# Another order for the table of portions in the second block of a fused two-block transformer kernel

## What is computed

```
h = rmsnorm(x, attn_norm)
c_q, c_kv, k_r, q_d, k_d, v_d = split(h @ w_in)      # 384, 256, 32, 512, 512, 512 columns
q  = rmsnorm(c_q)  @ w_uq        # 8 latent heads of 96
kv = rmsnorm(c_kv) @ w_ukv       # k (64) and v (64) of each; 32 rotated columns of k come from k_r
o_a = softmax(rope(norm(q)) rope(norm(k))^T) v        # 8 latent heads
o_b = dilated attention over q_d, k_d, v_d with a relative bias   # 8 dilated heads
x = x + concat(o_a, o_b) @ w_out
x = x + conv_ffn(rmsnorm(x))
```

## Time and profile before

| | |
|---|---|
| runs | 1645.78, 1648.69, 1649.99 us; median 1648.69 |
| profiled execution | 1644.55 us, span 1642.8 us |
| TensorE matmul / weight load | 1589.0 us (97%) / 1463.2 us (89%) |
| VectorE / ScalarE / GpSimd | 1129.8 us (69%) / 919.0 us (56%) / 127.2 us (8%) |
| first dense matmul of the table to T0 | layer 0: 993.7 to 1116.7 us; layer 1: 1320.3 to 1443.3 us |

### The profile page before, as it was taken

How to read it: one execution, slowest core, us unless ns; L and a number is a source line. 1 busy time by engine, 2 the same in 40 slices (tenths; PEclk the granted TensorE clock), 3 DMA queues, 4 the chain that set the end, 5 groups by cost and what they waited for, 6 DMA issues and landing times. The chain is left out here.

```text
span 1642.8 us, 31046 instructions
## 1 busy us (share of the span) xinstructions
PE 1589.0 (97%) x12874; PEld 1463.2 (89%) x12874; DVE 1129.8 (69%) x1763; ACT 919.0 (56%) x1459; POOL 127.2 (8%) x106
## 2 busy tenths in 40 slices
PE   6999999999999999999999999999999999999999
PEld 3987478999999999966899999878999998799999
DVE  2799677645566655897765556778887567788873
ACT  3444756545365444647554446767666467676662
POOL 0230000112001100300011000000101000001110
PEclk9999999999999999999999999999999999999999
DMA  9443666656546555435566653323555533245553
GB/s 395 160 152 131 258 236 227 235 216 240 192 167 221 205 188 201 155 125 207 195 228 237 220 184 119 118 78 130 207 191 202 204 112 116 77 137 200 207 193 118
DMA packets 46172, 303.36 MB, mean 185 GB/s; under 512 B 5072, under 2 KB 7376, under 8 KB 12752
## 3 DMA queue, kind: packets, MB, share of 16 engines
q1 hardware_dynamic: 45312, 299.78, 50.7%
q0 software_dynamic: 288, 0.92, 0.1%
q10 hardware_dynamic: 432, 0.68, 0.1%
HBM read 298.22 MB, written 3.15 MB: 183 GB/s over the span
## 5 line engine op out<-in xcount | busy, mean ns | idle before, releaser
L2002 DVE TENSOR_TENSOR wl<-raw,wh 128x1040 fp32r<-128x1040 f32 (+1 forms) x472 | 576.4, 1260 | 295.8 <-ACT wh L1759 229.9
L1759 ACT ACTIVATE wh<-raw 128x1040 fp32r<-128x1040 f32 (+1 forms) x472 | 466.5, 1031 | 195.5 <-PE bank L1552 109.3
L1547 PE MATMUL bank<-hx_hi,wh 128*128 128x256 f32 x1856 | 519.6, 280 | 6.0 <-ACT hx_hi L1759 3.8
L1552 PE MATMUL bank<-hx_lo,wh 128*128 128x256 f32 x1856 | 516.2, 278 | 0.0
L1550 PE MATMUL bank<-hx_hi,wl 128*128 128x256 f32 x1856 | 514.7, 277 | 0.3 <-DVE wl L2002 0.2
L1547 PEld LDWEIGHTS bank<-hx_hi,wh 128*128 128x128 f32 x1856 | 349.0, 188 | 10.8 <-issue 9.8
L1550 PEld LDWEIGHTS bank<-hx_hi,wl 128*128 128x128 f32 x1856 | 349.1, 188 | 2.8 <-issue 1.7
L1552 PEld LDWEIGHTS bank<-hx_lo,wh 128*128 128x128 f32 x1856 | 348.8, 188 | 1.0 <-DVE hx_lo L1995 0.4
L1550 PE MATMUL bank<-hid_hi,wl 128*128 128x256 f32 x912 | 252.2, 277 | 1.4 <-DVE wl L2002 1.4
L1547 PE MATMUL bank<-hid_hi,wh 128*128 128x256 f32 x912 | 252.5, 277 | 0.3 <-ACT wh L1759 0.2
L1552 PE MATMUL bank<-hid_lo,wh 128*128 128x256 f32 x912 | 251.9, 276 | 0.0
(11 more groups left out here) (218 smaller groups left out, 1891.5 us busy)
## 6 DMA issues: line engine op xcount, KB each, us to landing
raw<-in_wts SPq DMA_DIRECT2D x208, 1032.0 KB, 4.9
raw<-in_wts SPq DMA_DIRECT2D x50, 1024.0 KB, 6.6
raw<-in_wts SPq DMA_DIRECT2D x20, 776.0 KB, 4.3
raw<-in_wts SPq DMA_DIRECT2D x4, 584.0 KB, 4.4
tscr<-tmp SPq DMA_DIRECT2D x4, 512.0 KB, 7.4
bias<-tscr SPq DMA_DIRECT2D x4, 512.0 KB, 6.0
raw<-in_wts SPq DMA_DIRECT2D x2, 648.0 KB, 4.0
xTc<-in_ctxT SPq DMA_DIRECT2D x1, 1024.0 KB, 10.6
```

Source lines behind the costliest of these rows:

```text
L1547: pe.matmul(out, block(f, M.wh, w0 + k, ncols, c, m), x_hi, start=first and k == 0 and o == 0, stop=False, skip_group_check=True)
L1552: ins = pe.matmul(out, block(f, M.wh, w0 + k, ncols, c, m), x_lo, start=False, stop=last and k == nk - 1, skip_group_check=True)
L1759: return act.activation(out, in_, func, bias=bias, scale=scale)
L2002: tt(M.wl[k][:, cols], M.raw[r][:, cols], M.wh[k][:, cols].bitcast(F32), ALU.subtract).then_inc(*on.inc(lo))
```

## The change

Only the table `BETWEEN` changes; no step is added or removed.

```diff
-BETWEEN = ("h r D0 h L0 L2 N r r D2 D4 r D3", "", "D1 r r Q0", "K0", "", "s K1 h s V Q1", "r r", "s r D5 h h", "h r",
-           "Q3 Q2 h", "", "s K2 r r r K3 h", "s", "r O0 h O1 s", "", "O2", "", "h O3 h", "h", "h s T0 T1 T2 T3 h")
+BETWEEN = ("h r D0 h D2 r L0 r", "L2 N D4", "D3 r", "D1 r r Q0", "K0 s r", "r Q1", "K1 r h", "r D5 r h", "V h",
+           "Q2 K2 h", "r r Q3 h", "K3 r r O0 h", "O1 s", "h", "O2 h", "h", "O3 h", "h", "h", "h s T0 T1 T2 T3 h")
```

## The result

The kernel after takes 1707.05 us (median of 4 runs, 1705.25 to 1709.36), before 1648.3 beside it: ratio 1.0358, 95% interval 1.034 to 1.0377. The prediction said slower and had the direction, but its size was half of what came: +30.3 us forecast (1679 on 1648.69), +58.7 measured, and 1707 lies outside the range of 1663 to 1694.

The account below looks back on a forecast made before the run. Matmuls bound the kernel, so only TensorE's waits can change. Five steps sum to 17.2 us a layer, taken as 15.0, plus 0.7 for the clock; twice 15.7 is 31.4, forecast 1679 us, range 1663 to 1694.

Parts of the forecast that it names:

- Scores 0: Row 0: scores come right behind D2's rest, so TensorE waits for q and k; +2.2 us a layer.
- Latent rest: Rows 1 to 3: moved behind D3, it makes TensorE wait, mostly 7.4 us for D1's square; net +6.4 us a layer.
- Rows 4 to 10: Spread Q and K work makes turned 3 wait about 3.5 us, less 2.2 for double rests; net +1.9 a layer.
- O0's split: Row 11: O0's piece is split only directly ahead of its matmuls; 4.0 us wait less 2.8, net +1.2 a layer.
- The tail: Rows 12 to 18: dense pieces in even rows leave turns 13, 15, 17 waiting; net +5.5 us a layer.
- second rival: Whole table: queues clear during row 3's wait, so later waits shrink; about +8 us a layer, 1665 us; chance 0.17.
- clock term: Behind the 7.4 us wait for D1's square the clock falls once a layer, half hidden; +0.7 us a layer.
- first rival: The clock falls at every wait over 3 us (D1's square, turned 3, O0, turned 15); 1690 us; chance 0.12.
- waits overlap more: Turned 3 and the tail wait less since queues clear in row 3; about +8 us a layer, 1665; chance 0.17.
- the latent rest finds its cover: Row 3: D1's square is not held up, so removed waits decide; -2 to -4 us a layer, 1642; chance 0.03.
- it cancels: Whole table: the queues catch up everywhere and the kernel stays within its old waits, 1649 us; chance 0.04.
- A: Experiments' theory, D0 to T0: clock falls cost time of their own beside the waits, some 8 to 10 us a layer.

Follow-up runs that it names:

- e5: The new table with D2's rest ahead of L0 instead of behind it (row 0): 1698.42 us, ratio 1.0315 to the kernel before.
- e6: The new table with 18 constant matmuls a layer added in the long TensorE waits, each fill meant to be shorter than its wait: 1699.22 us, ratio 1.031.
- e12: The new table with 7 constant matmuls added in the wait at D1's small matmul alone: 1703.10 us, ratio 1.034.
- e1: The new table with the latent rest back directly behind N, ahead of D4 and D3 (rows 1 and 2): 1690.22 us, ratio 1.0266.
- e8: The new table with rows 11 to 18 in the old order, D2's rest ahead of L0 and the latent rest directly behind N: 1659.67 us, ratio 1.007.
- e7: The new table with rows 11 to 18 in the order of the kernel before: 1684.36 us, ratio 1.0215.
- e2: The new table with O0 one row later (row 12), so its piece can be split ahead: 1708.21 us, ratio 1.0375.
- e9: The kernel before with double rests and O0 spread as in the new table (rows 9 to 13): 1648.54 us, ratio 1.0006.
- e4: The new table with 38 constant matmuls a layer added in seven long TensorE waits: 1707.40 us, ratio 1.037.
- e11: The kernel before with O2 moved to row 14 and O3 to row 16: 1654.34 us, ratio 1.0045.

## Why the prediction missed the size

**By steps, layer 0.**

1. *Scores 0*: right. 2.2 forecast, 2.28 measured; e5 shows it can be had back by cover alone.
2. *Latent rest*: right. D1's square 7.4 against 6.95, PSUM 1.2 against 1.42. The 1.1 at scores 2 isn't there: with the clock at 0.50 Q0 took 4.6 us (2.5 in the kernel before), and the product was ready. At full clock it is 0.2 (0.18 in e6, 0.16 in e12), so the term was too large in any case. e1 takes the step back and wins what it says (6.4 forecast, 7.6 and 6.5).
3. *Rows 4 to 10*: turned 3 waited 2.29, forecast 3.5, the 0.6 behind it did not come. The 2.2 that was subtracted for the double rests was never a wait, so the net of +1.9 came near the 2.3 measured by luck. e8 has 4.0 us of waits more than the kernel before: 2.3 at turned 3, the rest in rows 1 to 3 (1.1) and the tail (0.6).
4. *O0's split*: 4.0 forecast, 2.40 + 1.43 measured: right. What was set against it, 2.8 in row 11, was 1.2. The reason, a split that starts too late, is borne out by e7, where the piece is whole before O0 and 0.59 is left; e2, which has only half of it split ahead, gains nothing.
5. *The tail*: 2.2, 2.6, 3.4 forecast, 1.95, 2.24, 1.69 measured, and 0.73 for values 7 as said. The last was half of its forecast: VectorE had nothing queued by then (1.55 us idle ahead of the split half at 1142.14), which is what the second rival had right.
6. *T0 to T3*: forecast untouched, 1.1 us longer in layer 0, by the fall that the last waits left behind.

**The two steps that failed.** Against 15.7 us a layer stand 28.6 measured (mean of both): 18.5 of waits, 8.8 of clock and 1.4 of rest. The waits were 3.5 short (2.2 of it because I took 15.0 for the 17.2 that the list gave), the clock 8.1, and the rest, whose cause stays open, was not forecast at all. The new waits came to 29 by my list and to 23.3 by the trace. The first failing step is the *subtraction*: 11.8 us of waits were to go with the old table (3.4 in rows 1 to 3, 2.2 for the double rests, 2.8 in row 11, 3.4 in the tail), but there were only 5.0 in it (1.0, 0, 1.2 and 2.8). The prediction added up a layer from start-to-start times, got 106 us and called the missing 14 to 17 "waits and hand-overs". The list of waits, which gives 5.0 in four lines, was not weighed against that sum; with the busy 118.0 it makes up the 123.0, so the busy column hid no wait. Part of the error lay in the 512-column f32 matmuls of the rests: their price was read as the distance to the next record (1025.38 to 1025.83), while the pair takes 0.86 us. The stretch has 12 of them, which makes 5 of the 12 us between 106 and 118.0. Another part may be the dense pieces: the stretch holds 480 such matmuls, ten times 48 with O0 to O3, and the sum names eight; as it isn't written out, this stays open. The 3.26 us of the latent rest are work (14 records, two of them D0's rest, and no gap in the list of waits), not 1.8 of work and 1.4 of wait, and e9 moves the double rests for nothing. Overcounts on both sides happened to cancel, which is luck: 17.2 net forecast (15.0 taken), 18.3 measured.

The second, and the one that made the miss, is the *clock term*: 0.7 us a layer forecast, 9.6 and 8.0 measured. I put one fall behind the longest wait alone and took half of it as hidden. In layer 0 five came, at waits of 1.7 to 7 us, each of 3 to 10 us, and TensorE was busy for some 19 us of the layer at 1.2 GHz; layer 1 had four. That is my first rival's mechanism, with a chance of 0.12, but it too counted only waits over 3 us, at 1.5 us each; the 1690 that it gave was 17 us short. Its argument against (before holds 1.00 through waits of 1 us) said nothing of waits of 2. The Trainium skill (TensorE: Matmul & The Clock Gate, Part 1) says that the throttled state is the default and activity releases it; the falls at turned 13 and 15 agree with it, more than I let it count, while turned 3, with 2.29 us, had none.

**The rivals.** That waits overlap more (1665) was right for the tail and turned 3 and worth 6 us a layer of new waits, offset by the 7 us of waits that were falsely subtracted. That the latent rest finds its cover (1642) is out: the chain took 9.8 us. That it cancels is out; the `h` of rows 7 to 10 are indeed no-ops in both (the `s` of row 7 before is not: it makes the split at 1066.25).

**What was only bounded.** The loss at half clock is an upper bound of what it costs. Taken back, 6.9 us of it gave 4.8 (e6), and waits and fills together grew by 1.6: the two half splits of ScalarE at 1052.89 took 1.99 us within the fall, as long as at full clock (2.00 at 1037.23 in the kernel before), so a TensorE that comes sooner waits longer for the other engines. That falls cost time beside the waits, A's mechanism, is shown by e4, e6, e7 and the first layer of e11; the size that A gave them, 8 to 10 us a layer, is not. From e6, about 70% of the 8.8 us mean loss, 6 us a layer, is what the clock really cost, and waits and rest make the other 22 to 23 (an estimate).

## What to carry to other kernels

Before subtracting a wait, find it in the list of waits of the kernel before: a sum of instruction prices that falls short of the stretch can be work that was priced too low, as part of it was here, and not a wait. For a change of order, count the TensorE work between handing something to ScalarE or VectorE and asking for it back, and put the queue of both engines into that time; that gave each new wait to about 1 us here, the last one in the tail to 1.7. Then price the clock: where new waits of about 2 us came here, a half-clock stretch of 3 to 7 us followed most of them, 10 us with the longest. It cost about a quarter of the waits on top of them (6 of 23 us a layer, an estimate), and in the tail up to nearly as much as the waits (5.1 against 5.7 in layer 0 of e7, 3.4 against 6.2 in layer 1). And take a move of cover alone before several together: K1 beside K0 gave 0.9 us a layer, the set that held it lost 4.6.

## What the runs showed of the hardware that was not expected

- The granted clock fell to 0.50 behind waits as short as 1.69 + 0.73 us (turn 15 and values 7) and 1.95 us (e11_tail_alone, layer 0), but not behind 2.29 us at turned 3, 1.94 us at the same turn in e11's layer 1, or 0.71 + 1.77 us (values 4 and turn 10) in e7. The same 2.33 us at scores 0 in e12 had a fall in layer 1 and none in layer 0, and turned 3, which held in both layers of after, had a fall in both layers of e1 and e5 with 2.3 us of wait. Layer 1 of after has four falls, none at scores 0. Length alone doesn't decide it; what does stays open, and no run varied one thing alone to find it.
- Three of the five falls in layer 0 begin within the wait (at 1050.8, 1112.2 and 1136.1), and TensorE works 3 to 6 us at half rate before the clock is back. These show as **busy**: TensorE's busy time in layer 0 rose from 118.0 to 128.8 with the same matmuls. The Trainium skill (Perfetto Trace Analysis, Identifying the Most-Contended Engine) distrusts matmul busy time and trusts weight-load busy as a measure of how close a kernel is to its limit; here both rose (weight load from 101.5 to 109.2), so at a changing clock neither is a measure of work.
- A 512-column f32 matmul leaves two records of 0.43 us, 0.86 in all at full clock; the first record's start-to-start distance is half its price.
- Matmuls on constants in a long wait hold the clock at 1.00 (e4) and win 8 us of 1707 when they are shorter than the waits (e6), nothing when they are longer (e4).
